# Eight row buffers instead of four, and TensorE's merge tiles written out, in a decoder block on one core

## The reference

```
xn  = RMSNorm(h);  q,k,v (two kinds), g_a, g_b = split(xn @ W_in)
y_a = sliding-window attention      y_b = stick-breaking attention     (1024 x 512 each)
h   = h + (sigmoid(g_a) * (y_a @ P_a) + sigmoid(g_b) * (y_b @ P_b)) @ W_o
h   = h + MoE(RMSNorm(h))           top-4 of 32 experts
expert: (min(g,7), clip(u,-7,7)) = x @ W_gate_up[e] + b;  ((u+1) * g*sigmoid(1.702 g)) @ W_down[e] + b
```

## Time and profile before

| | |
|---|---|
| three runs | 2784.26, 2788.34, 2789.40 us; median 2788.34 |
| the profiled execution | 2779.78 us, span 2778.4 us |
| mean granted TensorE clock | 0.95 |
| TensorE matmuls | 2548.2 us busy, 92% of the span |
| chain that ended last | PE L1670 36%, PE L1684 18% |
| merge stage, from the first row transfer to the last split's end | 798 to 925 us |
| experts | 1128 to 2750 us |

### The profile page before, as it was taken

How to read it: one execution, slowest core, us unless ns; L and a number is a source line. 1 busy time by engine, 2 the same in 40 slices (tenths; PEclk the granted TensorE clock), 3 DMA queues, 4 the chain that set the end, 5 groups by cost and what they waited for, 6 DMA issues and landing times.

```text
span 2778.4 us, 45432 instructions
## 1 busy us (share of the span) xinstructions
PE 2548.2 (92%) x17728; PEld 2343.2 (84%) x17729; DVE 872.7 (31%) x1950; ACT 671.0 (24%) x1543; POOL 506.3 (18%) x636
## 2 busy tenths in 40 slices
PE   6989999999979891699999999999999999999996
PEld 6767767687767681699999999999999989999995
DVE  3034443535334313223323223232323223222322
ACT  3254554645433210011111111111111111111110
POOL 1301101010111004212212212121212212211211
PEclk9989999999989995799999999999999999999998
DMA  3101102011133423788989889999999879877993
GB/s 121 31 17 29 54 25 65 21 47 45 56 118 124 157 107 102 237 262 272 284 267 279 277 262 295 303 291 309 286 309 277 279 226 281 262 253 235 287 308 86
DMA packets 439680, 524.03 MB, mean 189 GB/s; under 512 B 33170, under 2 KB 347596, under 8 KB 439500
## 3 DMA queue, kind: packets, MB, share of 16 engines
q1 hardware_dynamic: 401580, 475.40, 52.1%
q0 software_dynamic: 26464, 42.72, 7.3%
q10 hardware_dynamic: 11520, 4.20, 0.6%
HBM read 478.90 MB, written 47.56 MB: 189 GB/s over the span
## 4 chain that ended last, share of the span: by engine, by line
PE 57%; issue 3%; DMA 0%; POOL 0%; DVE 0%; POOLq 0%; ACTq 0%; ACT 0%
PE ex_gu L1670 36%; PE ex_yp L1684 18%; PE ex_tr L1638 1%; PE ex_tr L1650 1%; DMA ex_hid<-in_b_gate_up_dram 0%; PE ex_tr L1657 0%; DMA ex_hid<-in_b_down_dram 0%; POOLq L1333 0%; POOL acc_s L1506 0%; POOL acc_s L1510 0%; DVE ex_xT L1574 0%; DVE ex_ytok L1581 0%; DVE ex_ytok L1585 0%; DVE ex_bT L1561 0%; ACTq L1387 0%
## 5 line engine op out<-in xcount | busy, mean ns | idle before, releaser
L1670 PE MATMUL ex_gu<-ex_xT,ex_w 128*128 128x136 f32 (+1 forms) x8192 | 1025.6, 287 | 40.2 <-issue 40.2
L1670 PEld LDWEIGHTS ex_gu<-ex_xT,ex_w 128*128 128x128 f32 x8192 | 1014.9, 192 | 41.8 <-issue 41.8
L1684 PE MATMUL ex_yp<-ex_hid,ex_w 128*128 128x136 f32 (+1 forms) x4096 | 513.3, 285 | 0.0
L1684 PEld LDWEIGHTS ex_yp<-ex_hid,ex_w 128*128 128x128 f32 x4096 | 503.4, 190 | 0.0
L1455 ACT ACTIVATE ex_sg<-ex_g 128x160 f32<-128x160 f32 x256 | 86.2, 337 | 1061.1 <-DVE ex_g L1599 1061.1
L1599 DVE TENSOR_SCALAR ex_g<-ex_gu,ex_bcur 128x160 f32<-128x160 f32 x256 | 98.3, 384 | 648.6 <-PE ex_gu L1670 648.6
L55 PE MATMUL at_job<-xnT_hi,at_whi 128*128 128x512 f32 x448 | 195.1, 435 | 0.0
L1460 ACT ACTIVATE ex_yT<-ex_yp,ex_bcur 128x128 f32<-128x128 f32 x256 | 94.0, 367 | 390.0 <-PE ex_yp L1684 390.0
L602 POOL TENSOR_TENSOR at_wlo<-at_raw,at_whi 128x1024 fp32r<-128x1024 f32 x32 | 79.5, 2485 | 580.4 <-ACT at_whi L447 580.4
L56 PE MATMUL at_job<-xnT_lo,at_whi 128*128 128x512 f32 x448 | 179.4, 400 | 0.0
L57 PE MATMUL at_job<-xnT_hi,at_wlo 128*128 128x512 f32 x448 | 179.3, 400 | 0.0
(11 more groups left out here) (220 smaller groups left out, 2832.2 us busy)
## 6 DMA issues: line engine op xcount, KB each, us to landing
ex_w<-in_w_gate_up_dram SPq DMA_DIRECT2D x256, 1024.0 KB, 7.7
ex_w<-in_w_down_dram SPq DMA_DIRECT2D x128, 1024.0 KB, 7.2
at_raw<-in_w_in_dram SPq DMA_DIRECT2D x28, 512.0 KB
gT<-at_gst SPq DMA_DIRECT2D x32, 256.0 KB, 2.2
mg_g<-gT SPq DMA_DIRECT2D x32, 256.0 KB, 3.1
n_x<-in_x_dram SPq DMA_DIRECT2D x8, 512.0 KB, 8.1
mg_ytok<-y_s SPq DMA_DIRECT2D x16, 256.0 KB, 2.9
raw_o<-in_w_out_dram SPq DMA_DIRECT2D x8, 512.0 KB, 6.7
```

The source lines that it names most:

```text
L1670: last = nc.tensor.matmul(gu[:, ft % 4, 256 * part:256 * part + width], w_tile(ft // 2, ft % 2, k, part), xT[:, k, 0:width], start=k == 0, ...
L1684: last = nc.tensor.matmul(yp[:, dt % 2, 0:width], w_tile(4 + dt // 4, dt % 4, k), hid[:, k, 0:width], start=k == 0, stop=k == KD - 1)
```

## The change

`ytok` gets eight buffers and eight arrival semaphores in place of four; the transfer of number n waits for the transposes of number n-8. TensorE alone no longer goes through `over_tiles`: its eight tiles are written out. The other engines keep their loop.

```diff
-        ytok = sb("mg_ytok", [P, 4, HALF])
+        ytok = sb("mg_ytok", [P, 8, HALF])
...
-        y_in = [sem(f"mg_y_in{s}") for s in range(4)]
+        y_in = [sem(f"mg_y_in{s}") for s in range(8)]
...
-                    after(sp, tr_mm, n - 3)
-                    sp.dma_start(ytok[:, n % 4, :], y_s[a, t * P:(t + 1) * P, :]).then_inc(y_in[n % 4], 16)
+                    after(sp, tr_mm, n - 7)
+                    sp.dma_start(ytok[:, n % 8, :], y_s[a, t * P:(t + 1) * P, :]).then_inc(y_in[n % 8], 16)
...
-                    pe.wait_ge(y_in[n % 4], 16 * (n // 4 + 1))
+                    pe.wait_ge(y_in[n % 8], 16 * (n // 8 + 1))
...
-                over_tiles(pe, body)
+                for m in range(KD):
+                    body(m, m % 2, m < KD - 1)
```

More of the change, by code:

```diff
@@ L996, in _ @@
                     t, a = divmod(n, 2)
-                    pe.wait_ge(y_in[n % 4], 16 * (n // 4 + 1))
+                    pe.wait_ge(y_in[n % 8], 16 * (n // 8 + 1))
                     after(pe, ylo, n - 3)
                     for k in range(4):
-                        last = nc.tensor.transpose(tr[:, n % 4, k * P:(k + 1) * P], ytok[:, n % 4, k * P:(k + 1) * P],
+                        last = nc.tensor.transpose(tr[:, n % 4, k * P:(k + 1) * P], ytok[:, n % 8, k * P:(k + 1) * P],
                                                    ident[:, :])
```

## The result

The changed kernel takes 2741.5 us (median of 4 runs, 2737.1 to 2746.8), the kernel before beside it 2786.3 us (2777.4 to 2789.4): ratio 0.984, 95% interval 0.982 to 0.986. That is 44.8 us less, where 49.1 were forecast, and 2.5 us above the predicted 2739.

What follows compares the result with a forecast made beforehand. TensorE was taken as the bound, stalling for code in the expert loop. Terms of -45, -1.4 and -2.7 sum to -49.1 us, from the 2788.3 median to 2739; 8-in-10 range 2731 to 2778.

Steps and rivals of the forecast that it cites:

- The stalls: Expert loop: five TensorE waits for code at jumps back vanish when it spans seven 256-instruction blocks, not eight; -45 us.
- the second stall: First expert's wide body: the 1.43 us code wait after 48 instructions goes, as the first boundary comes 180 instructions in.
- The idle part: Expert loop: TensorE's waiting in the five stalls at the jump back, 30.8 us, would be saved.
- the first stall: Start of the first expert: a 7.99 us wait on jumping over unfetched code blocks, forecast to stay.
- from above: Expert stage: 23 narrow experts at 46.65 us and 9 wide at 54.1, set against the measured stretch; 47.8 us to gain.
- The fitted piece: Expert loop's last block, entered 11 instructions before the jump back: the harmful next-block fetch is dropped in five of seven wide passes.
- three, none, two, four: Expert loop: code packets fetched in a wide expert, the next expert, the jump back and after it, repeating around all five stalls.
- The eight buffers: Merge stage: attention rows and first weights arrive sooner at 300 GB/s, so TensorE starts earlier; -2.7 us, bounds 0 to 4.
- The written-out part: TensorE's merge part: removing the loop is worth 0, bounds 0.6 us gained or 1.6 us either way.
- The fetch pattern stays: Rival for the expert loop: stalls remain and only the merge stage gains, 2785.6 us; chance 0.09.
- The loop test on the wrong side of a border: Rival for the expert loop: it still spans eight blocks, seven stalls instead of five, 2804 us; chance 0.08.
- Weights as the new bound: Rival in the experts: DMA, at a share of 0.95, binds once stalls give no slack; no separate time or chance.

Runs made afterwards that it cites:

- e3: Kernel before plus 112 idle semaphore increments on TensorE ahead of the expert loop, which then spans seven code blocks: 2747.6 us, ratio 0.986.
- e4: Kernel before plus 111 idle increments on TensorE ahead of the expert loop, which then spans eight code blocks: 2820.3 us, ratio 1.012.
- e8: Changed kernel plus 130 idle increments ahead of the expert loop, putting it back in eight code blocks: 2783.6 us, ratio 1.000.
- e1: Kernel before with eight buffers alone, TensorE's loop over column tiles kept: 2777.9 us, ratio 0.998.
- e2: Kernel before with TensorE's merge part written out alone, four buffers kept: 2750.4 us, ratio 0.987.
- e6: Changed kernel plus 60 idle increments ahead of the expert loop, still seven code blocks: 2738.0 us, ratio 0.984.
- e9: Kernel before with eight buffers and 190 idle increments ahead of the expert loop (seven code blocks), loop over column tiles kept: 2735.5 us, ratio 0.982.
- e10: Kernel before plus 60 idle increments ahead of the expert loop, eight code blocks, the last entered some 70 instructions before the jump back: 2778.9 us, ratio 0.998.
- e11: Kernel before plus 112 idle increments placed behind the expert loop, where they move nothing in it: 2802.8 us, ratio 1.007.
- e7: Changed kernel with the two expert bodies exchanged in TensorE's code, the wide one first: 2735.4 us, ratio 0.983.
- e12: Kernel before with eight buffers, 190 idle increments ahead of the expert loop, and the wide body placed ahead of the narrow: 2734.6 us, ratio 0.982.

## Why the prediction was right

**The stalls (-45).** Right in mechanism, count and size. With the 1.4 of the second stall the forecast for the expert stage was -46.4; it lost 45.4 us in the two profiles (1617.4 and 1572.0 us, from the first load of a count to the loop's exit). The idle part was 31.4, for 30.8 + 1.43 forecast, less 0.8 by which the first stall grew (7.99 to 8.78); the half-clock part was 14.1 for 11.7. That the position decides, and not what the change says it does, is shown by e3 against e4, by e8, and by e1 against e2. Where a loop of seven blocks gave no second-expert stall, the stage took 1571 to 1572 us in four kernels (the changed one twice, e6, e9); with the stalls 1610 to 1617 in five (before, e1, e8, e10, e11). By the means of the two groups the gain is 42; the 45 leans on a profiled execution that had five stalls. The estimate "from above" was 2.7 us too high in itself: a wide expert takes 54.35 us in the changed kernel, not the 54.1 that the count of matmuls gave, and with 54.35 and 46.67 its 47.8 would be 45.1.

**The fitted piece** was that in five of seven wide passes the fetch of block 45 is dropped. It had to be fitted because it is not a rule: at the same layout, or one two instructions off it (e8), the profiles have four stalls (e1) or five (before, e8, e11), behind different experts. Nor do the packets come as "three, none, two, four" around all five stalls of the kernel before. They do around three. Behind the stall at 2223 us one came and then three in the next expert (the row of four in the earlier trace rows is from the stall after it), and at the last one the wide expert's own jump stalled, with no expert in between. The prediction didn't need either, since at seven blocks no jump back stalled in any of the eight traces.

**The Trainium skill** (Runtime: NRT & Kernel Launch, Instruction fetch mechanics) says that a jump outside two pages of 256 instructions stalls. The trace disagrees: 28 jumps back in a row over seven blocks, the first at the end of the fourth expert, bring no packet and no wait in the changed kernel. Its sentence that crossing a border is mostly hidden holds for straight code here: behind the first stall no other wait stands in the first expert, which crosses three borders. It does not hold at a jump back over eight blocks.

**The second stall (-1.4).** Right in the changed kernel. What the prediction did not see is that another may stand one expert later, in e2 and e3: 4.5 us of wait, and 6 to 7 us more for the stage than in the changed kernel. It may be what the changed kernel's runs at 2746.8 have; no trace of one shows it, and why it comes in some executions is open.

**The eight buffers (-2.7).** The step was right, its size too small: 3.9 us in the two profiles. Over all traces TensorE started 23.4 to 25.4 us after the first row's issue in six kernels with four buffers, and 19.0 to 20.8 in eight with eight. The mean difference is 4.0, the bound that was worked out from 344 GB/s. While the rows came in, 338 GB/s flowed in the changed kernel (803 to 816 us) and 258 before (799 to 816 us), so 300 was the wrong choice between the ends.

**The written-out part (0).** Right, within what e9 against e6 can tell.

**The sum.** Against the profiled execution the forecast was 2730.7, and the profiled one took 2737.05. The parts close: attention +4.1 (the merge stage begins at 802.36, not 798.28), start of the merge matmuls -3.9, from there to the first load of a count +2.6 (310.6 for 308.0), expert stage -45.4, behind it -0.1, together -42.7, as measured. The first and third of these lie within the scatter: in the other traces the stage begins at 796.9 to 803.1 us, and the profiled execution of before was an early one. The prediction knew that it lay 8.6 us below its median and forecast from the median, and that is why 2739 was 2.5 us off and not 6. Some of that is luck: of the 4.3 us that the gain fell short (44.8 for 49.1), 2 were made up by the median of the three runs shown, 2788.3, which lay that much above the one that the kernel before had beside the changed one, 2786.3.

**The rivals.** "The fetch pattern stays" is what e1 and e8 are. "The loop test on the wrong side of a border" is e4: of the seven stalls that it counted six stand at a jump back and one at a branch, and their price over the kernel before was 35 us where it took 18. Weights as the new bound did not come: no wait of TensorE for them behind the first stall, at a DMA share of 0.95 over 454 us.

## What to carry to other kernels

Waits put down to "issue" that recur at one loop's head are worth a look at the queue of kind "instruction": if packets come in pairs at the jump back, count the instructions of the loop body and where its first and last stand in blocks of 256. A loop that touches eight blocks and could touch seven is cured here by moving its start, with harmless instructions in a stretch where the engine waits anyway (e3, 38 us less), and any edit ahead of such a loop, whatever it is for, must be timed as a move of the loop too. So compare a change with its own length in idle instructions before its gain is put down to what it says it does.

## What the runs showed of the hardware

One TensorE instruction more or less ahead of a loop of 1,661 instructions changed the time by 72.7 us of 2,780 (e3, e4). A semaphore increment on TensorE took 0.15 us (e11). A first jump over code that was never fetched costs a wait of 7.4 to 8.8 us, and putting the code first that is run first moves the wait to the next such jump, where it is 4.1 to 4.2 us (e7, e12). A jump back that waits for its block takes 4.9 to 5.1 us with one packet in it (e10), 6.5 to 7.4 us with two (the kernel before), and where its target is the last instruction of a block 5.7 to 6.5 us more follow (e4). Behind the five stalls of the kernel before the granted clock was 0.50 (1.2 GHz) for some 5 us, in the first for part of it, and the expert behind a stall took 1.6 to 3.0 us more than one without: so much comes on top of the wait that the profile lists.
